# One key product for two heads, and a reordering of the prologue, the change of layers and the operand copies of an attention pair

## The reference, cut to what matters

```python
def mla_kv(zckv, zkr, g, w_ukv, tabs):
    kv = (rms_norm(zckv, g) @ w_ukv).reshape(B, L, MLA_HEADS, MLA_NOPE + MLA_V)   # 6 heads, 64 + 64
    k_nope, v = jnp.split(kv, [MLA_NOPE], axis=-1)
    ...
    k = jnp.concatenate([k_nope, jnp.broadcast_to(k_pe, (B, L, MLA_HEADS, MLA_ROPE))], axis=-1)
def hybrid_layer(...):
    hl = layer_norm(xl) * (1 + sc_l) + sh_l
    z = hl @ p["w_in"]                 # and the same for the context
    ...                                # three families of attention
    y_l = merge_groups(o_a, o_b, o_m, ga_l, gb_l, gc_l, p["w_out"])
    xl_new = layer_norm(DEEPNORM_ALPHA * xl + gt_l * y_l, p["ln_g"], p["ln_b"])
```

## Time and profile before

| | us |
|---|---|
| three runs | 966.56, 968.30, 972.94 (median 968.3) |
| the profiled execution | 967.27, its span 965.5 |
| TensorE busy in the span | 923.2 (96%) |
| VectorE, GpSimd, ScalarE busy | 565.5, 511.2, 430.2 |
| granted TensorE clock, mean | 0.987 |

### The profile page before, as it was taken

How to read it: one execution, slowest core, us unless ns; L and a number is a source line. 1 busy time by engine, 2 the same in 40 slices (tenths; PEclk the granted TensorE clock), 3 DMA queues, 4 the chain that set the end, 5 groups by cost and what they waited for, 6 DMA issues and landing times.

```text
span 965.5 us, 13483 instructions
## 1 busy us (share of the span) xinstructions
PE 923.2 (96%) x4699; PEld 665.4 (69%) x4699; DVE 565.5 (59%) x900; ACT 430.2 (45%) x877; POOL 511.2 (53%) x431
## 2 busy tenths in 40 slices
PE   5999999999999999999999799999999999999996
PEld 4678667889655665665678589888984555565684
DVE  5469133513687669962228838667257757884346
ACT  5331221413565466655234852235344545664432
POOL 3137223324687645565546517455438875466672
PEclk9999999999999999999999999999999999999998
DMA  9957672214533200020453202322352311020252
GB/s 321 279 209 242 217 244 78 76 39 100 133 70 80 50 17 18 18 66 1 146 177 113 81 16 77 87 81 82 83 121 63 71 46 25 9 74 10 85 178 88
DMA packets 51754, 95.85 MB, mean 99 GB/s; under 512 B 9508, under 2 KB 24720, under 8 KB 50664
## 3 DMA queue, kind: packets, MB, share of 16 engines
q1 hardware_dynamic: 51688, 94.99, 32.4%
HBM read 71.32 MB, written 4.21 MB: 78 GB/s over the span
## 4 chain that ended last, share of the span: by engine, by line
PE 83%; DVE 9%; ACT 4%; POOL 2%; issue 2%; DMA 0%; POOLq 0%; SPq 0%; ACTq 0%; DVEq 0%
PE banks L982 15%; PE banks L984 14%; PE banks L983 14%; PE banks L1250 12%; PE banks L1272 11%; PE banks L1225 6%; PE banks L993 2%; PE banks L1291 2%; PE banks L1284 1%; DVE negmax L2183 1%; DVE area_b L2352 1%; PE banks L1123 1%; PE banks L1387 1%; DVE scr L2349 1%; ACT late_bias L1768 1%
## 5 line engine op out<-in xcount | busy, mean ns | idle before, releaser
L1899 POOL TENSOR_TENSOR w_split<-w_raw,w_split 128x512 fp32r<-128x512 f32 (+4 forms) x121 | 147.7, 1230 | 224.4 <-ACT w_split L1515 224.4
L982 PE MATMUL banks<-w_split,area_a 128*128 128x512 f32 (+3 forms) x606 | 230.5, 380 | 9.0 <-DVE area_a L2393 6.8
L984 PE MATMUL banks<-w_split,area_a 128*128 128x512 f32 (+3 forms) x606 | 223.0, 368 | 0.0
L983 PE MATMUL banks<-w_split,area_a 128*128 128x512 f32 (+3 forms) x606 | 222.4, 367 | 0.0
L2183 DVE TENSOR_REDUCE negmax<-banks 128x1 f32<-128x768 f32 x160 | 149.2, 952 | 80.1 <-PE banks L1225 79.7
L1515 ACT ACTIVATE w_split<-w_raw 128x512 fp32r<-128x512 f32 (+4 forms) x121 | 68.5, 580 | 192.2 <-PE banks L984 185.4
L1627 ACT ACTIVATE area_z<-banks 128x512 f32<-128x512 f32 x196 | 108.8, 598 | 80.0 <-PE banks L1250 76.6
L982 PEld LDWEIGHTS banks<-w_split,area_a 128*128 128x128 f32 x606 | 114.5, 189 | 41.0 <-issue 19.1
L1250 PE MATMUL banks<-area_a 97*128 97x512 f32 (+4 forms) x448 | 129.0, 399 | 4.4 <-ACT area_z L1627 3.1
L984 PEld LDWEIGHTS banks<-w_split,area_a 128*128 128x128 f32 x606 | 114.5, 189 | 16.7
L983 PEld LDWEIGHTS banks<-w_split,area_a 128*128 128x128 f32 x606 | 114.8, 189 | 12.8
(11 more groups left out here) (224 smaller groups left out, 1475.0 us busy)
## 6 DMA issues: line engine op xcount, KB each, us to landing
w_raw<-in_w_in_dram SPq DMA_DIRECT2D x32, 512.0 KB, 4.6
area_g<-in_w_ada_dram SPq DMA_DIRECT2D x13, 1024.0 KB, 6.3
area_g<-in_w_ada_dram SPq DMA_DIRECT2D x16, 512.0 KB, 4.8
w_raw<-in_w_out_dram SPq DMA_DIRECT2D x16, 512.0 KB, 4.5
area_a<-parts SPq DMA_DIRECT2D x72, 96.0 KB, 2.2
area_a<-parts SPq DMA_DIRECT2D x30, 192.0 KB, 3.6
area_b<-in_x_dram SPq DMA_DIRECT2D x8, 512.0 KB, 7.4
w_raw<-in_w_in_dram SPq DMA_DIRECT2D x8, 352.0 KB, 3.3
```

Source lines behind the costliest of these rows:

```text
L982: nc.tensor.matmul(dst, a[0], b[0], start=first, stop=False)
L983: nc.tensor.matmul(dst, a[0], b[1], start=False, stop=False)
L984: return nc.tensor.matmul(dst, a[1], b[0], start=False, stop=last)
L1899: op = nc.gpsimd.tensor_tensor(lo, raw, hi.bitcast(F32), ALU.subtract)
```

## The change

The columns of `ukv` are laid out as six keys, then six values. The key product is made only with an odd unit and takes 128 columns that hold the keys of both heads; an even unit keeps its query alone. ScalarE still makes four key copies for two heads, now all of them behind the odd unit's product. `mla_high` of an odd unit moves behind step 3 and `copy_maxrow`, that of an even unit to the end of the pair before; `copy_latents` goes behind step 1. The maxima wait for the high parts alone (`mla_hi`), the scores of step 0 for the low ones. VectorE's `mla_low` of an odd unit comes one `reduce_max` later. GpSimd's first sum in pair 1 waits for VectorE's last sum of pair 0. The prologue loads and turns tile 4 earlier, turns tile 5 after the second half of the first quarter, and turns a quarter by four transposes and a reduction on VectorE in place of the products with `pick`. At the change of layers two slices are held instead of three, in memory that is free earlier (`ukv` and the end of `parts`), and the splits and copies of tiles 1 to 4 change places on VectorE and ScalarE.

```diff
-HELD = [("in", 1, CHUNK_ORDER[0], k) for k in (3, 4, 5)]
+HELD = [("in", 1, CHUNK_ORDER[0], k) for k in (3, 4)]
-def mla_parts(L):
-    return [("q", 1), ("k", 1)] + ([("q", 0)] if L < DEPTH - 1 else []) + [("k", 0)]
+def mla_parts(L, u):
+    groups = (1, 0) if L < DEPTH - 1 else (1,)
+    if u % 2 == 0:
+        return [("q", g) for g in groups]
+    return [("q", 1), ("k", 1)] + [("q", g) for g in groups[1:]] + [("k", 0)]
...  sync
-            for t in range(4):
+            for t in range(5):
                 load_x(t)
             load_quarter(0, 0)
-            load_x(4)
             load_x(5)
...  where the slices lie, and what they wait for
+        def held_slice(k):
+            flat = (ukv if k == 3 else parts)[:].rearrange("p a n -> p (a n)")
+            at = 0 if k == 3 else 2048
+            return [flat[:, at + i * 512:at + (i + 1) * 512] for i in range(2)]
             elif s in HELD:
-                eng.wait_ge(filled, USE["y", s[1] - 1, 1, out_tiles(s[1] - 1)[-1]] + 1)
+                scored(eng, s[1] - 1, NPAIR - 1)
...  tensor: turn_quarter, mla_head, max_tile, scores, the start
-                for i in range(2):
-                    for w in range(2):
-                        at = w * 256 + i * P
-                        mm = nc.tensor.matmul(banks[:, 6, 4 * i + 2 * w:4 * i + 2 * w + 2], ada_rows[:, q % 2, at:at + P],
-                                              pick[:], start=True, stop=True)
+                for b in range(4):
+                    mm = nc.tensor.transpose(banks[:, 6, b * P:(b + 1) * P], ada_rows[:, q % 2, b * P:(b + 1) * P], ident[:])
-                        mm = three(dst, [ukv[:, i, h * P:(h + 1) * P] for i in range(2)],
+                        mm = three(dst, [ukv[:, i, (h - 1) * 64:(h + 1) * 64] for i in range(2)],
                     if family(u) == "mla":
-                        pe.wait_ge(mla_lo, N_MLA[L, u])
+                        pe.wait_ge(mla_hi, N_MLA[L, u])
                 if step == 0:
                     pe.wait_ge(mrow_in, 32 * (PN[L, p] + 1))
+                    if head_pair(p):
+                        pe.wait_ge(mla_lo, N_MLA[L, 2 * p + 1])
-                    for t in range(4):
+                    for t in range(3):
                         turn_x(L, t)
                     ada_half(0, 0)
+                    turn_x(L, 3)
                     turn_x(L, 4)
+                    ada_half(0, 1)
                     turn_x(L, 5)
-                    ada_half(0, 1)
                     turn_quarter(0)
...  scalar: mla_copy, mla_high, attend, finish
+                        copy(qk_t[0:64, 2 * ((m - 1) % 2) + 1, tokens(g)], src[0:64])
+                        op = copy(qk_t[0:64, 2 * (m % 2) + 1, tokens(g)], src[64:128])
                     exponent(L, p, 0)
-                    if context:
-                        copy_latents(L, p - 1)
-                    if head_pair(p + 2):
-                        mla_high(L, 2 * p + 4)
                     exponent(L, p, 1)
+                    copy_latents(L, p - 1)
                     if context:
                         copy_context(L, p - 1)
-                    else:
-                        copy_latents(L, p - 1)
-                    if head_pair(p + 2):
-                        mla_high(L, 2 * p + 5)
                     exponent(L, p, 2)
                     copy_denominators(L, p - 1)
                     exponent(L, p, 3)
                     copy_maxrow(L, p + 1)
+                    if head_pair(p + 2):
+                        mla_high(L, 2 * p + 5)
...
                     if context:
                         exponent(L, p, "ctx")
+                    if head_pair(p + 3):
+                        mla_high(L, 2 * p + 6)
...
+                split_w(HELD[0])
                 square_rows("new", L, ts[0])
-                for n in range(1, len(ts)):
+                split_w(HELD[1])
+                for n in range(1, len(ts) - 1):
...
+                square_rows("next", L, ts[4])
+                modulate_next(L + 1, ts[2])
+                square_rows("new", L, ts[5])
+                next_row(L, ts[4])
+                modulate_next(L + 1, ts[3])
+                square_rows("next", L, ts[5])
+                modulate_next(L + 1, ts[4])
+                next_row(L, ts[5])
+                modulate_next(L + 1, ts[5])
...  gpsimd: sum_probs, finish
                     if step == 1 and p == 1:
                         pool.wait_ge(w_lo, N_SLICE["uq", L, 0, 0])
+                        pool.wait_ge(dve_summed, N_DVE_SUM[L, 0, 1])
-                        if n == len(ts) - 1:
+                        row_root("new", L, ts[n])
+                        if n == 0:
                             split_w(HELD[0])
                             split_w(HELD[1])
-                        row_root("new", L, ts[n])
-                    split_w(HELD[2])
...  vector: attend, finish, quarter_columns, prologue
+                    reduce_max(L, p + 2, 1)
                     if head_pair(p + 2):
                         mla_low(L, 2 * p + 5)
-                    reduce_max(L, p + 2, 1)
                 for n, t in enumerate(ts):
+                    if n == 5:
+                        split_next(ts[1])
                     gained_tile(n, t)
-                    if n > LAG:
-                        split_next(ts[n - LAG - 1])
+                    if n == 4:
+                        split_next(ts[0])
+                    elif n == 5:
+                        split_next(ts[2])
                     new_row(n, t)
-                for t in ts[-LAG - 1:]:
+                for t in ts[3:]:
                     split_next(t)
+                strips = banks[:, 6, :].rearrange("p (b j r) -> p b r j", b=4, j=4)[:, :, 0:2, :]
+                chain(nc.vector.tensor_reduce(strip_sum[:], strips, AX.X, ALU.add))
-                    dve.wait_ge(pool_const, 1)
-                    nc.vector.tensor_reduce(pick[:], ident[:].rearrange("p (j r) -> p r j", j=4)[:, 0:2, :], AX.X, ALU.add)
                     rows_in(3)
+                    rows_in(4)
                     scale_rows(3)
-                    rows_in(4)
                     rows_in(5)
```

More of the change, by code:

```diff
@@ L949, in w_views @@
             if kind == "ukv":
-                return [(flat[:, 0:768], ukv[:, 0, :], ukv[:, 1, :])]
+                src = flat[:, 0:768].rearrange("p (h z n) -> p z h n", h=6, z=2)
+                hi, lo = (ukv[:, i, :].rearrange("p (z h n) -> p z h n", z=2, h=6) for i in range(2))
+                return [(src[:, z], hi[:, z], lo[:, z]) for z in range(2)]
             src = flat[0:UQ, 0:576].rearrange("p (h n) -> p h n", h=6)
```

51 lines of the change are left out of this document (22 added, 29 removed).

## The result

The changed kernel takes 958.4 us in the median of four runs (955.8 to 960.9) against 967.4 of the kernel before beside it: ratio 0.990, interval 0.9869 to 0.9930. So 9 us were gained and 19 to 20 forecast.

A forecast was written before the change was run, and what follows sets the result against it. TensorE, busy 923.2 of 965.5 us, was taken as the bound. Latent pairs 11.0, GpSimd waits 1.6, change of layers 4.9 and prologue 2.5 sum to 20.0 us off 967.3: 947.3, median 948.3, range 942 to 957.

The forecast's parts named there:

- operand copies: Latent pairs 5 and 6: moving ScalarE's copies ends TensorE's waits, 4.2 us idle, 6.3 in all; moved copies priced at nothing.
- its cap: Latent pairs 5 and 6: VectorE's free time limits the gain to 4.4 us in layer 0, 4.5 in layer 1.
- Keys: Latent pairs: one key product for two heads saves TensorE 1.05 us a head, 6.3 us for six heads.
- Layer 0's whole term: Latent stretch of layer 0: merged keys and moved copies together, forecast to gain 5.45 us.
- Layer 1's: Latent stretch of layer 1: merged keys and moved copies together, forecast to gain 5.55 us.
- Prologue: Before the first projection: earlier start of its products and cheaper quarter turns, 2.5 us, from 0.5 to 3.5.
- Last sums: Pairs 0 and 1: GpSimd waits so VectorE's last sums run unstretched, 1.6 us, from 0 to 2.
- Change of layers: Between layers 0 and 1: tile 1 split earlier, two slices held, slice 6 sooner by 4.9 us, from 2 to 7.
- the second forecast: Rival: VectorE bounds the latent pairs, so pairs 5 and 6 give 3 us, not 8.9; 955.6 us, chance 0.22.
- ScalarE didn't come late: Rival, latent pairs: moved copies delay exponents by 4.4 us a pair; 975 us, chance 0.03.
- Full clock: Rival: the trace's four half-clock stretches may go, 1.7 us each, with upper ends of the terms; 942 us, chance 0.10.
- The gains are hidden: Rival: what TensorE saves it waits for elsewhere; 960 to 968 us, chance 0.10 for 958.6 to 978.

The follow-up runs named there:

- e3: The changed kernel with two-head keys, but operand copies, the odd split and the old waits back at their old places: 954.4 us, ratio 0.9855.
- e4: The kernel before with the change of layers, the prologue and GpSimd's wait, without merged keys or moved copies: 957.7 us, ratio 0.9893.
- e2: The changed kernel, with GpSimd's first sum of a pair waiting for VectorE's split of the even unit's operands: 955.3 us, ratio 0.9866.
- e5: The changed kernel with merged keys in both layers, but moved copies, and GpSimd's first sum waiting for the even split, in layer 0 alone: 950.6 us, ratio 0.9831.
- e7: The kernel before with only GpSimd's wait for VectorE's last sums in pair 1 added: 966.4 us, ratio 0.9986.
- e10: e5 with the copies moved in layer 1 too, and there the even split directly behind reduction 7: 949.6 us, ratio 0.9786.
- e11: e4 with the moved copies added, so the changed kernel with the old key products: 963.0 us, ratio 0.9915.
- e1: The changed kernel, with VectorE's even split moved behind reductions 7 and 8, in front of the odd split: 959.9 us, ratio 0.9915.
- e12: e10 with VectorE's last sum of the even unit moved behind reduction 4 in layer 1: 952.6 us, ratio 0.9850.
- e6: e2, with GpSimd's sums of step 4 also waiting for the even unit's rotation: 963.1 us, ratio 0.9964.

## Why the prediction was wrong

**The step that failed** is that of the operand copies, with its cap. It said that the waits for ScalarE go (they did: no score at step 2 or 3 waits), that the moved copies fit and cost nothing, and that VectorE's free time bounds the gain, "24.94 - 22.01 = 2.9" and so on. The last was the fault. Free time in a window says how much work would fit, not whether the next reduction comes in time. What had to be followed was VectorE's list from the moved copy on: the even split would start at once, GpSimd's sums would start 1.9 us earlier in the pair, the split would be stretched from its first instruction, and a reduction stands behind it. Every number for that was in the trace: the earlier trace rows have the stretching, and I used it for two other parts of the change. The prediction named a delay of "up to 1 us a pair", for the odd split; it was the even one, whose place in the list had not changed. Only its neighbours in time had. In layer 1 the next query's rotation, in front of the split, is stretched as well, and the term had counted on 1.6 us of half clock going with the old waits, where 3.4 us more of it came.

Two readings of the prediction were off without deciding anything. "0.69 against 4.23 us" sets one sum against two, which alone take 1.4. And VectorE left 2.6 us in pair 6 of layer 0 (24.92 less 22.28), not 2.9.

**Keys** measured 4.7 for the 6.3 asked, without the half clock, three quarters. In layer 0 they gave 2.1 for 3.15: TensorE's idle time there is 3.1 us in e3 and 2.5 in e4, with new waits of 0.49 and 0.23 us for `negmax`. **Layer 0's whole term** of 5.45 is there (6.0 in e2 and e5) once GpSimd waits. **Layer 1's** isn't: the best is 4.3 of 5.55, with the copies unmoved (87.98 to 83.68, of which 1.6 are the half clock that e7 shows to go by itself). VectorE's busy time in that stretch is 69.05 us before, 69.26 with the keys (e3 and e5) and 73.44 after, for the same instructions: 4.2 us of stretching that the move makes. In layer 0 it is 79.24 and 79.37; there it isn't more stretching that harms, but where it falls.

**Prologue**: 2.3 for 2.5 in these two profiles. The first projection product is at 24.57, forecast 24.2; the 0.91 and 1.73 us of idle time in front of it didn't go, they are one gap of 2.65 now, and the 0.9 us come from what stands before. **Last sums**: 0.9 for 1.6. The 0.71 us for the denominators went, and layer 1's two sums take 1.70 (1.4 forecast) for 4.23 in the earlier trace rows. At the start of pair 1 in layer 1 the kernel is 0.8 us ahead by this, and 0.4 of it is lost again in the next pair. Of the thirteen runs with GpSimd's wait, four have 3.4 us of half clock here (after, e3, e5 and e7) and take 65.05 to 65.10 us to the turn in pair 4; the nine others take 64.4.

```profile
727.06 1.70 DVE L2232 TENSOR_TENSOR w_raw<-w_raw,late_bias 128x512 f32<-128x512 f32 x2
```

**Change of layers**: 2.9 in this pair of profiles, 2.9 to 4.4 in all of them, forecast 4.9 and 2 to 7. The waits of the new order came close to their prices: the turn of the last tile 1.34 (1.9), the third slice's place 0.70 (0.85). Half clock is gone in this profile; five of the eleven runs with the new order have 3.4 us of it here, and are no longer for it. TensorE's rows answer to the earlier trace rows:

```profile
540.88 0.47 PE L992 MATMUL banks<-w_split,area_a 128*128 128x512 f32 x1 [0.76 <-issue]
545.30 0.50 PE L992 MATMUL banks<-w_split,area_a 128*128 128x512 f32 x1 [2.11 <-DVE area_a L2407]
557.58 1.09 PE L1050 MATMUL banks<-ident,vals 128*128 128x128 f32 x8 [1.34 <-ACT vals L1790]
```

What is missing is at tile 1. TensorE goes on with it at 545.30, which is 550.3 with the 5.0 us added that were gained before layer 0's last turn; the prediction had 548.6. Its split starts 1.6 us late by the same count, and stands behind a row that waited 0.99 us for GpSimd's root, which I had not followed:

```profile
541.77 1.29 DVE L2393 SCALAR_TENSOR_TENSOR area_b<-o_t,row_std,area_g 128x1024 f32<-128x1024 f32 x1 [0.99 <-POOL row_std L1933]
...
543.29 0.69 DVE L2406 CAST area_a<-area_z 128x1024 fp32r<-128x1024 f32 x1
544.02 1.23 DVE L2407 TENSOR_TENSOR area_a<-area_z,area_a 128x1024 fp32r<-128x1024 f32 x1
```

The held splits on GpSimd, 516.1 to 519.6, did stretch a VectorE instruction, but by 0.9 us and not by the 2.8 that I had weighed: the first new row took 2.23, where the next takes 1.28.

```profile
516.20 2.23 DVE L2393 SCALAR_TENSOR_TENSOR area_b<-o_t,row_std,area_g 128x1024 f32<-128x1024 f32 x1 [0.80 <-POOL row_std L1933]
...
522.78 1.28 DVE L2393 SCALAR_TENSOR_TENSOR area_b<-o_t,row_std,area_g 128x1024 f32<-128x1024 f32 x1 [1.06 <-POOL row_std L1933]
```

At the next tile VectorE waits for GpSimd's root all the same, 1.06 us, so the stretching isn't seen any more there. Slice 6 begins at 569.60 for 578.09; without the 5.0 us from before, 3.5 are gained there, where 4.9 were forecast. 2.9 are left at layer 1's first turn. Most of the rest is lost in one place late in the projection, where the first maxima wait for the DMA of their operands, which they didn't before (no wait there in e4, e10 and e11, 0.5 us in e3):

```profile
689.68 0.58 PE L1232 MATMUL banks<-area_a 96*128 96x384 f32 x2 [0.32 <-DMA area_a<-ones_r]
```

**The rivals.** The engine of the second forecast, VectorE as the bound of the latent pairs, was right, its mechanism (the list is full) only in part and its price, 955.6, too kind. ScalarE didn't come late in the changed kernel (in e1 it did). "Full clock" didn't come: outside the last stretch both profiles have 17.1 us of half clock. "The gains are hidden" is in part what happened in the latent pairs, 6.7 us of new waits for 4.2 of old ones, and 958.4 is just under its range. All three signs that I had named as wrong appeared: TensorE waiting for `negmax`, pairs of 25.2 and 23.6 us in layer 0, and half clock in new places.

**Open.** Whether layer 1 can have keys and moved copies both without a gap: e10 removes one collision and meets the next, e12 a third. e10's stretch of 85.34 contains 6.8 us of half clock; at 1.6 for each 3.4 that is an estimate of 82.1 without it, under the 83.7 of e3 and e5. No run shows it: e12 has no half clock there and takes 86.13.

## What to carry to other kernels

When a wait is taken away, list for each engine what now starts earlier and what it will run beside; a wait of one engine can be what keeps two others apart. A bound by busy time holds only for the sum; follow the list of the next engine to the first instruction that someone waits for, and price what stands in front of it as it runs beside its new neighbour. An engine that is held back may run its list without pauses later, and what starts beside it then can stand for the whole row (5.41 us in e2 and e6). And two edits that are each worth nothing (a move, and a wait that protects it) can be worth 4 us together, so parts are to be tried in pairs as well as alone.

## What the runs showed of the hardware

VectorE's subtractions and additions between tiles in SBUF, and its split of 96x768, take 0.7 to 0.96 us alone and mostly 1.65 to 2.05 beside a GpSimd sum, which itself takes 1.27 alone and up to 2.1 then; some beside a sum still take 0.69 (802.98 in the changed kernel). When GpSimd ran four sums without a pause, a VectorE instruction with two inputs in SBUF took 5.41 us, as long as the four and itself (e2 at 846.98, e6 at 408.52). VectorE's reductions out of PSUM stay at 0.94 to 0.96 beside the same sums (354.64 and 801.99 in the changed kernel). The Trainium skill ("SBUF — State Buffer", section "SBUF: two separate sides") has a lock of the shared port for VectorE instructions with two SBUF inputs, and by it the reductions are free; the trace agrees.

Half clock can follow a short gap, but the length of the gap doesn't decide it. In the changed kernel the granted clock fell to its lower level, 1.2 GHz, for 3.4 us from 356.3, just behind an idle time of 1.45 us, and not behind one of 1.37 at 380.9; in e10 it fell for 6.8 us behind one of 1.47. But in e1 it fell behind one of 1.33 (361.87) and not behind one of 1.96 (417.32), and in e11 not behind 1.44 and 1.47 in layer 0. The gap of 2.09 to 2.11 us at the change of layers has half clock at it in five of the eleven runs that have that gap. A stretch of 3.4 us costs 1.6 us in layer 1 (87.98 with one and 86.34 without, before and in e7), as much as the gap that it follows, so two single profiles are compared only with the half clock of each beside them.
